# Sparse attention's score and value products paired on TensorE's halves; maximum before scaling in two softmax pipelines

## The reference, cut to what matters

```python
def block(start):                       # 128 queries
    s = einsum('bhqd,bhkd->bhqk', qb, kh) + cb[..., :, None] - cum[:, :, None, :]
    a = softmax(where(causal_mask(start, T), s, NEG_INF))
    return einsum('bhqk,bhkd->bhqd', a, vh)
```

## Time and profile before

| | us |
|---|---|
| median of 3 runs | 3703.51 (3692.9 to 3707.81) |
| profiled execution | 3702.44 |
| its span | 3700.7 |
| TensorE busy | 3361.9 (91%) |
| VectorE busy | 2018.4 (55%) |
| ScalarE busy | 1299.6 (35%) |
| GpSimd busy | 374.7 (10%) |

### The profile page before, as it was taken

One profiled execution on the slowest core, in us unless ns is written; L12 is line 12 of the kernel. 1 busy time (PEld: TensorE's weight loads), 2 busy tenths in 40 slices (PEclk: granted clock), 3 DMA queues, 4 the chain that ended last, 5 costly groups with the idle time before them and its releaser, 6 DMA issues.

```text
span 3700.7 us, 51884 instructions
## 1 busy us (share of the span) xinstructions
PE 3361.9 (91%) x21498; PEld 2638.2 (71%) x21498; DVE 2018.4 (55%) x3571; ACT 1299.6 (35%) x2143; POOL 374.7 (10%) x334
## 2 busy tenths in 40 slices
PE   6898899999898999998987889888999889999998
PEld 4667777777685677786766666566777777777886
DVE  5455356653433466655546345578877862455443
ACT  3233232222223332223432134455555532424221
POOL 0001000000000000000001000045444520000000
PEclk9898899999998999999997989999999989999999
DMA  3120024441551134432220120121111102232321
GB/s 125 60 69 1 24 91 131 133 135 59 94 94 35 52 97 137 137 108 91 92 69 18 59 80 7 40 88 39 40 43 42 50 6 86 74 114 91 103 94 66
DMA packets 318856, 274.78 MB, mean 74 GB/s; under 512 B 10912, under 2 KB 310048, under 8 KB 317856
## 3 DMA queue, kind: packets, MB, share of 16 engines
q1 hardware_dynamic: 314368, 256.07, 22.9%
q10 hardware_dynamic: 4256, 15.40, 1.1%
HBM read 265.16 MB, written 6.29 MB: 73 GB/s over the span
## 4 chain that ended last, share of the span: by engine, by line
PE 77%; DVE 13%; ACT 5%; issue 3%; DMA 1%; POOL 1%; DVEq 0%; ACTq 0%; SPq 0%; POOLq 0%
PE ps L95 75%; DVE f L107 4%; DVE f L101 3%; DVE r L101 3%; PE ps L98 2%; ACT f L88 2%; DVE f L104 1%; ACT r L92 1%; ACT L88 1%; POOL f L101 1%; DVE f L113 1%; ACT f L92 1%; DVE f L110 1%; ACT f L89 0%; DVE r L107 0%
## 5 line engine op out<-in xcount | busy, mean ns | idle before, releaser
L95 PE MATMUL ps<-r,r 128*128 128x512 f32 x10368 | 2462.1, 396 | 124.9 <-DVE r L101 88.8
L95 PEld LDWEIGHTS ps<-r,r 128*128 128x128 f32 x10368 | 1927.2, 190 | 604.7 <-issue 183.6
L95 PE MATMUL ps<-f,f 64*64 64x64 f32 (+10 forms) x10192 | 859.2, 271 | 170.7 <-issue 45.5
L101 DVE TENSOR_TENSOR r<-f,r 128x1024 fp32r<-128x1024 f32 (+2 forms) x621 | 657.0, 1063 | 464.0 <-ACT r L92 456.3
L95 PEld LDWEIGHTS ps<-f,f 64*64 64x64 f32 (+3 forms) x10192 | 631.9, 158 | 371.4 <-issue 173.1
L92 ACT ACTIVATE r<-f 128x1024 fp32r<-128x1024 f32 (+2 forms) x548 | 506.6, 937 | 783.3 <-PE ps L95 661.3
L92 ACT ACTIVATE f<-ps 128x256 f32<-128x256 f32 (+3 forms) x422 | 184.7, 453 | 616.1 <-PE ps L95 365.1
L101 POOL TENSOR_TENSOR f<-f,f 128x256 f32<-128x256 f32 (+1 forms) x276 | 331.3, 1213 | 485.1 <-ACT f L88 273.3
L107 DVE SCALAR_TENSOR_TENSOR f<-f,f,f 128x128 f32<-128x128 f32 (+3 forms) x622 | 365.2, 592 | 26.5 <-ACT f L88 7.3
L101 DVE TENSOR_TENSOR f<-ps,f 128x512 f32<-128x512 f32 (+7 forms) x333 | 180.2, 553 | 337.3 <-PE ps L95 328.0
L88 ACT ACTIVATE f<-ps 128x512 f32<-128x512 f32 (+3 forms) x203 | 112.0, 553 | 628.5 <-PE ps L95 626.5
(11 more groups left out here) (33 smaller groups left out, 743.0 us busy)
## 6 DMA issues: line engine op xcount, KB each, us to landing
f<-in_w_mlp_up SPq DMA_DIRECT2D x32, 1024.0 KB, 6.1
f<-in_w_mlp_down SPq DMA_DIRECT2D x32, 1024.0 KB, 6.0
f<-in_w_ff SPq DMA_DIRECT2D x32, 1024.0 KB, 5.3
f<-in_w_ada SPq DMA_DIRECT2D x48, 512.0 KB, 4.0
f<-in_w_in SPq DMA_DIRECT2D x24, 1024.0 KB, 4.9
f<-in_w_in SPq DMA_DIRECT2D x44, 512.0 KB, 3.5
f<-in_w_in_even SPq DMA_DIRECT2D x12, 1024.0 KB, 5.1
f<-in_w_in_odd SPq DMA_DIRECT2D x12, 1024.0 KB, 12.5
```

The lines of the kernel that those rows point to most:

```text
L95: return self.e.matmul(out, l, r, start=first, stop=last)
L101: return self.e.tensor_tensor(out, a, b, op)
```

## The change

`turns(n, order)` is like `waves`, but the phases of a round come in the order given, and only those named.

- Fox: VectorE's order in a round becomes phase 0 (row), 1 (maximum of r - 1), 2 (scaling of r - 2), 5 (output). ScalarE's becomes 1 (exponential of r - 1), 3 (copy of r - 3). TensorE's is as before.
- Nsa: the same, with the output and the rest behind: VectorE 1, 2, 5; ScalarE 1, 3. TensorE keeps 5, 4, 3, 2, 1, 0.
- Nsa, TensorE: scores of heads h and h + 1 are issued together in the round of the even head, one on rows 0 to 63, one on rows 64 to 127; values of heads h - 1 and h together in phase 4 of the odd head, alternating over kt between the two column halves; the compressed unit's small products alternate between the halves.

```diff
-        for u, p in waves(32, 6):
+        for u, p in turns(32, (1, 3)):            # Fox.act
-        for u, p in waves(32, 6):
+        for u, p in turns(32, (0, 1, 2, 5)):      # Fox.dve
+def turns(n, order):
+    for r in range(n + max(order)):
+        for p in order:
+            if 0 <= r - p < n:
+                yield r - p, p
...
-        for what, u, p in self.rounds():
+        for what, u, p in self.rounds((1, 3, 5, 0)):   # Nsa.act; Nsa.dve has (1, 2, 5, 0), Nsa.pe (5, 4, 3, 2, 1, 0)
...
+                for j in range(4):
+                    for par in range(2):
+                        pp = slice(par * 64, par * 64 + 64)
+                        t = pe.mm(K.ps.t[self.bank["cs", qt, par]][:, j * 32:j * 32 + 32], self.q[pp, j, qs],
+                                  self.kc2[pp, j // 2, :], True, True)
...
+                if h % 2 == 0:
+                    for s in (self.soft(u), self.soft(u) + 1):
+                        pp = slice((h + s) % 2 * 64, (h + s) % 2 * 64 + 64)
+                        b = self.bank["s", s] = K.ps.take(pe, ("nsa_max", s + 1))
+                        K.mm_done(pe.mm(K.ps.t[b][:, 0:qs.stop], self.q[pp, h // 2, qs], self.k[br][pp, h // 4, 0:qs.stop], True,
+                                        True), ("nsa.s", s))
...
+                if h % 2 == 1:
+                    pe.wait_ge("nsa_pt", u + 1)
+                    b = self.bank["acc", qt]
+                    for kt in range(qt + 1):
+                        for w in (u - 1, u):
+                            pp = slice((h - u + w) % 2 * 64, (h - u + w) % 2 * 64 + 64)
+                            t = pe.mm(K.ps.t[b][pp, h // 2 * 128:h // 2 * 128 + 128],
+                                      self.v[br][:, kt, h // 4 * 64:h // 4 * 64 + 64],
+                                      self.pt[w % 3][:, kt * 128:kt * 128 + 128], False, br == 1 and h == 7 and kt == qt)
+                            if kt == qt:
+                                K.mm_done(t, ("nsa.o", w))
```

More of the change, by code:

```diff
@@ L2672, in soft, with rounds @@
         return u - u // 17 - 1
-    def rounds(self):
+    def rounds(self, order):
         last = -1
-        for u, p in waves(68, 6):
+        for u, p in turns(68, order):
             if u + p != last:
@@ L2753, in pe @@
         pe.fence()
-        for what, u, p in self.rounds():
+        for what, u, p in self.rounds((5, 4, 3, 2, 1, 0)):
             if what == "half":
@@ L2775, in pe @@
                 for par in range(2):
[L2776 to L2781, removed]
+                    self.bank["cs", qt, par] = K.ps.take(pe, ("nsa_cs", 2 * qt + par + 1))
+                for j in range(4):
[3 more added lines that the diff above has]
+                                  self.kc2[pp, j // 2, :], True, True)
+                        if j == 3:
+                            K.mm_done(t, ("nsa.cs", qt, par))
             elif br is None and p == 4:
@@ L2791, in pe @@
             elif p == 0:
[L2792 to L2795, removed]
-            elif p == 4:
[L2797 to L2802, removed]
+                if h % 2 == 0:
[4 more added lines that the diff above has]
+                                        True), ("nsa.s", s))
+            elif p == 4:
+                if h % 2 == 1:
[9 more added lines that the diff above has]
+                                K.mm_done(t, ("nsa.o", w))
             elif p == 5 and h == 7 and br == 1:
@@ L2854, in act @@
         act.fence()
-        for what, u, p in self.rounds():
+        for what, u, p in self.rounds((1, 3, 5, 0)):
             if what == "split":
@@ L2939, in dve @@
         k3 = lambda qt: self.gl[:, qt, :].rearrange("p (h j) -> p h j", j=3)
-        for what, u, p in self.rounds():
+        for what, u, p in self.rounds((1, 2, 5, 0)):
             if what == "split":
@@ L3009, in gps @@
         pool.fence()
-        for what, u, p in self.rounds():
+        for what, u, p in self.rounds((5, 0)):
             if what == "split" and self.sec.X.on_pool(u):
```

## The result

| | before | changed |
|---|---|---|
| median | 3705.28 us (3692.9 to 3707.81, 4 runs) | 3658.0 us (3654.93 to 3659.2, 4 runs) |
| ratio | | 0.9887, 95% interval 0.9871 to 0.9903 |
| profiled execution, its span | 3702.44, 3700.7 | 3657.74, 3655.9 |
| nsa | 189.2 | 148.7 |
| fox | 82.5 | 83.1 |

The change makes the kernel 1.1% faster; 3664 was predicted, with 3654 to 3680 as the range.

What follows compares the result with a forecast made beforehand. TensorE, busy 91% of the span, was taken to set the pace. Nsa's savings, 6.2 + 9.6 + 10.6 + 14.1 + 1.6 - 4.0 = 38.1 us, and fox's 0 turned 3702.4 into 3664, range 3654 to 3680.

Steps and rivals of the forecast that it cites:

- The pairs' price: On TensorE, two products on two halves, row or column, take the time of one.
- The loops: Nsa's third and fourth tiles: a pair of rounds takes 2.90 and 3.56 us, saving 10.6 and 14.1 us.
- By tile: Nsa's four query tiles: pairs of rounds save 6.2, 9.6, 10.6 and 14.1 us, before compressed unit and boundaries.
- The compressed unit: Nsa: alternating its 16 small instructions between halves saves 0.4 us each, 1.6 us for four.
- The boundaries: Start of nsa's third and fourth tiles: VectorE's chains of the compressed unit lose 2 us each, 4 us together.
- Fox: Fox stage: 0.71 us a head of row-tile wait removed, 0.6 of copy wait added, 0.8 at the end; together 0.
- Rival 1: Nsa hand-overs take more, each loop 0.6 us longer, 10 us in all: 3674; chance 0.09.
- rival 4: Clock falls to 1.2 GHz: in nsa's last part 32 us, 3696, chance 0.03; in all of it 3760, chance 0.02.
- rival 2: Column halves don't overlap in nsa's values pairs, costing 17.6 us: 3682; chance 0.05.
- rival 3: Neither kind of pair overlaps, as products wait on other semaphores; scores add 17 us more: 3699; chance 0.03.

Runs made afterwards that it cites:

- pairs alone: The changed kernel with VectorE and ScalarE back in their old orders in both stages, TensorE's pairs kept: 3675.76 us, nsa 169.8.
- orders alone: The changed kernel with TensorE's products unpaired as before, new VectorE and ScalarE orders kept: 3701.43 us (kernel before beside it 3699.46), nsa 194.4.
- copy first: The changed kernel with ScalarE's old order in both stages, copy ahead of the exponential: 3654.08 us, nsa 147.9, fox 78.5.
- row last: The changed kernel with fox's VectorE making the row tile last in the round: 3698.97 us, nsa 148.6, fox 119.1.

## Why the prediction was right

The profiled execution is 44.7 us shorter; by stretches: nsa 40.6, fox -0.7, all ahead of fox 4.7, between the stages -0.5, behind nsa 0.6.

- **The pairs' price: right.** Both halves' products take the time of one, row and column halves alike. The loop also needs VectorE's order: pairs alone gave 19.4 us, orders alone nothing, both 40.6; ScalarE's order has no part in it (copy first).
- **The loops: right.** n = 4: 3.56 predicted, 3.56 and 3.55 measured; n = 3: 2.90 and 2.91. TensorE waits 0.38 us in it (predicted 0.31; the rest is that eight transposes in a row take 1.02 us, not 2 x 0.59).
- **By tile**, the compressed unit and the boundary in it: predicted 6.6, 10.0, 9.0, 12.5 us; measured 6.2, 11.0, 9.6, 13.7. In the second tile a pair of rounds went from 6.10 us to a mean of 4.75: 1.35 saved, not 1.20. The products next to the filler got closer, too: two transposes ahead of a half tile take 0.19 us from start to start where two ahead of the scores had taken 0.37, and the half tile 2.83 instead of 2.95. Not every hand-over is covered by the filler, as the prediction had it: TensorE waits 0.30 and 0.34 us for a copy in two of the pairs.
- **The compressed unit:** sixteen small products 1.55 us before, 1.08 after: 0.47 each, 0.4 taken.
- **The boundaries: too dear.** 4 us taken. Loops and compressed unit give 10.6 + 0.5 and 14.1 + 0.5 for the last two tiles, of which 9.6 and 13.7 came: 1.5 + 0.9 = 2.4 lost. The waits are there (0.67 and 1.04 in the third tile, 1.53 and 0.79 in the fourth), but the loss is only six tenths of what was taken. These 1.6 us and the second tile's 1.0 are what the stage gained above 38.1.
- **Fox: right in kind and size.** Net 0 predicted; a head is 0.10 us shorter, 0.63 waited for the copy where 0.6 was predicted. The end costs 0.8 more as said (1.27 at 1233.79, against 0.47). The stage's 83.1 us against 82.5: its first two heads took 0.5 us more, the five periods behind them 0.5 less, the last head 0.7 more. The first two, in good part at 1.2 GHz, vary: the same kernel run again had 81.6.
- **Outside: not foreseen, and luck.** 4.7 us of the 6 between 3664 and 3658 were gained ahead of fox, where no code changed. Over the 13 profiles fox began between 1143.2 and 1158.5 us.

Rival 1 fell with the loop's length, rivals 2 and 3 with the x16 rows, rival 4 with the clock of 1.00. But the loss that rival 4 feared is real: the clock fell behind a wait in orders alone and, above all, in row last. What decides it stays open: in its last 30.4 us of nsa, pairs alone had TensorE busy for only 21.37 and a clock of 1.00. And one reading in rival 4 is wrong. The prediction says that fox's fp32 work alone did not raise the clock. It rose in the middle of that work: in the kernel before it was 0.50 from 1155 to 1172 us and 1.00 from there to 1243.6, with nothing but fp32 on TensorE.

## What to carry to other kernels

When two products that use one half of TensorE are paired, work out the loop that runs through the other engines' orders: here half of the gain came only because VectorE's maximum no longer stood behind a scaling, and the loop's length could be added up from the old profile to 0.01 us. A micro-order that removes a wait of TensorE can be worth far more, or less, than the wait, because the clock can change with it; compare stages within profiles, since unchanged code here moves the whole by more than the last few microseconds of tuning.

## What the hardware showed unexpectedly

- The column halves overlap though both use all rows. They overlap in part without alternating, too: the second half then starts when four instructions of the first are left (1.58 us for sixteen, against 1.09). The Trainium skill (TensorE: Matmul & The Clock Gate, Part 3, "What overlaps and what doesn't") has a sentence that lets weight loads overlap running matmuls only when the row groups differ; taken alone, as rival 2 took it, these runs disagree with it.
- Waits of 1.67 us, one in each of the last six heads, went with a mean clock of 0.66 in fox: 37.5 us more than the changed kernel run again (119.1 - 81.6), where the waits themselves are 6 x 1.67 = 10.0; a wait of 0.69 us at a tile's start (orders alone) preceded 4.8 us of loss, while one of 1.04 (the changed kernel) preceded none.
